# Eight neighbouring rows per partition for the expert up matrices, and a feed-forward input in permuted column order

## What is computed

```python
def route(h_flat, w_router, b_router):
    s = jax.nn.sigmoid((h_flat @ w_router).astype(jnp.float32))
    ...                                   # best group of 4, its 2 best experts, weights w
    return jnp.sum(jax.nn.one_hot(idx, N_EXPERTS, dtype=jnp.float32) * w[..., None], axis=1)

def moe(h, w_router, b_router, w1_l, w3_l, w2_l):
    ...
        a = jnp.einsum('td,edf->tef', xc, w1_l)     # d = 1024, f = 512, 16 experts
        b = jnp.einsum('td,edf->tef', xc, w3_l)
        u = jax.nn.silu(a) * b * gc[..., None]
        return jnp.einsum('tef,efd->td', u, w2_l)
...
        hx = rmsnorm(x, norm_ffn[l]) * (1 + sc_f) + sh_f
        x = x + g_f * moe(hx, w_router, b_router, w1[l], w3[l], w2[l])
```

## Time and profile before

| what | us |
|---|---|
| three runs | 1323.61, 1327.61, 1328.58 |
| median | 1327.61 |
| span of the profiled execution, first to last instruction | 1325.8 |
| PE busy | 1081.6 (82%) |
| DVE busy | 345.4 (26%) |
| ACT busy | 208.4 (16%) |
| queue of SP: share of the sixteen DMA engines | 58.9% |
| chain that ended last: PE 56%, DMA 29% (`ring<-in_w` alone 23%) | |

### The profile page before, as it was taken

One profiled execution on the slowest core, in us unless ns is written; L12 is line 12 of the kernel. 1 busy time (PEld: TensorE's weight loads), 2 busy tenths in 40 slices (PEclk: granted clock), 3 DMA queues, 4 the chain that ended last, 5 costly groups with the idle time before them and its releaser, 6 DMA issues.

```text
span 1325.8 us, 18500 instructions
## 1 busy us (share of the span) xinstructions
PE 1081.6 (82%) x6246; PEld 604.7 (46%) x6247; DVE 345.4 (26%) x812; ACT 208.4 (16%) x487; POOL 79.0 (6%) x126
## 2 busy tenths in 40 slices
PE   2799989988981999999899189989892898788771
PEld 1446447765450544444346044647642454344430
DVE  2201147565342100101011430157624011000002
ACT  1110023432010111111101211023300111011001
POOL 2000000001002000000000300000101000000001
PEclk8899999989985999999999689999985799999896
DMA  9923116576135899999369671313645699999993
GB/s 330 374 91 127 64 70 238 202 258 226 43 131 208 319 396 395 398 397 384 122 227 397 214 269 64 127 64 128 240 158 198 234 332 397 396 396 397 397 397 110
DMA packets 142294, 328.60 MB, mean 248 GB/s; under 512 B 6552, under 2 KB 8760, under 8 KB 142240
## 3 DMA queue, kind: packets, MB, share of 16 engines
q1 hardware_dynamic: 125424, 287.84, 58.9%
q0 software_dynamic: 7856, 25.61, 5.4%
q10 hardware_dynamic: 8960, 14.40, 3.1%
HBM read 308.10 MB, written 19.73 MB: 247 GB/s over the span
## 4 chain that ended last, share of the span: by engine, by line
PE 56%; DMA 29%; DVE 7%; ACT 3%; issue 3%; POOL 2%; SPq 0%; ACTq 0%; DVEq 0%; POOLq 0%
DMA ring<-in_w 23%; PE S L1217 17%; PE S L1398 10%; PE S L1327 6%; PE O L1281 4%; PE T L1155 3%; PE AUX L1172 3%; DMA ring<-in_w_ada 3%; PE S L1432 2%; PE T L1432 2%; PE S L1248 2%; PE S L1402 2%; ACT R L643 1%; PE S L1437 1%; DVE R L916 1%
## 5 line engine op out<-in xcount | busy, mean ns | idle before, releaser
L1217 PE MATMUL S<-ring,hT 128*128 128x512 f32 (+1 forms) x576 | 226.0, 548 | 2.3 <-ACT hT L587 2.3
L1402 PE MATMUL S<-ring,R 128*64 128x256 f32 x1472 | 181.1, 405 | 33.0 <-DMA ring<-in_w 28.3
L1402 PEld LDWEIGHTS S<-ring,R 128*64 128x64 f32 x1472 | 114.5, 146 | 106.3 <-DMA ring<-in_w 40.3
L1217 PEld LDWEIGHTS S<-ring,hT 128*128 128x128 f32 x576 | 108.0, 191 | 104.3 <-issue 98.6
L1398 PE MATMUL S<-ring,R 128*128 128x512 f32 x320 | 144.1, 610 | 6.5 <-issue 3.3
L1155 PE MATMUL T<-cst,R 128*128 128x128 f32 (+1 forms) x497 | 80.1, 292 | 64.2 <-DVE R L793 30.4
L1088 DVE SCALAR_TENSOR_TENSOR R<-R,S 128x256 f32<-128x256 f32 (+1 forms) x33 | 16.6, 502 | 412.7 <-ACT R L694 412.7
L1155 PEld LDWEIGHTS T<-cst,R 128*128 128x128 f32 (+1 forms) x497 | 60.2, 151 | 93.4 <-DVE R L793 30.7
L1398 PEld LDWEIGHTS S<-ring,R 128*128 128x128 f32 x320 | 62.1, 195 | 87.2 <-issue 82.4
L1437 PE MATMUL S<-ring,R 128*64 128x512 f32 x368 | 84.0, 598 | 9.6 <-DMA ring<-in_w 5.7
L1327 PE MATMUL S<-ring,hT 128*128 128x512 f32 x192 | 85.6, 607 | 2.3 <-issue 2.3
(11 more groups left out here) (143 smaller groups left out, 756.8 us busy)
## 6 DMA issues: line engine op xcount, KB each, us to landing
ring<-in_w SPq DMA_DIRECT2D x96, 2048.0 KB, 11.5
ring<-in_w_ada SPq DMA_DIRECT2D x24, 2048.0 KB, 8.1
ring<-in_w_in SPq DMA_DIRECT2D x8, 2048.0 KB, 10.8
R<-x_d POOLq DMA_DIRECT2D x45, 256.0 KB, 5.7
ring<-in_w_out SPq DMA_DIRECT2D x4, 2048.0 KB, 9.8
R<-mod_d SPq DMA_DIRECT2D x12, 512.0 KB, 9.6
y_d<-R ACTq DMA_DIRECT2D x46, 128.0 KB, 5.3
y_d<-R ACTq DMA_DIRECT2D x20, 256.0 KB, 6.5
```

The lines of the kernel that those rows point to most:

```text
L1217: ins = pe.matmul(S[:, i % 4, 0:width], hT[:, k, t * P:(t + 1) * P], w[:, k, :], start=(k == 0), stop=(k == KC - 1))
L1402: ins = pe.matmul(S[64 * h:64 * h + 64, i, 0:256], xT[:, half, k % 4, k // 4, 0:64], part[i][:, k, h * 256:h * 256 + 256], start=(k == 0), ...
```

## The change

Three edits. `expert_src` gives w1 and w3 with row 8p + k at partition p, place k: a partition gets eight neighbouring rows, one run of 16 KB. w2 is as it was. `wr` is loaded by the same rule, a run of 512 B per partition. And `ffn_input` writes hb so that column 128k + i holds feature 8i + k: it reads X, Af and Bf with a step of eight floats (32 B) and writes hb contiguously; the second operation reads hb contiguously. All that comes behind it (transposes, scatter, fetch, products) takes hb by chunks and is unchanged. X, Af, Bf and the output of the experts keep their order.

Each engine has the same instructions in the same order before and after. Only the shape of the SP loads of w1 and w3 (128x8x512 becomes 128x4096), that of the wr load (128x8x16 becomes 128x128), and the access patterns of L978 and L979 differ.

```diff
@@ expert_src @@
                 one = w[l, ds(e, 1)].rearrange("a k n -> (a k) n")
+            if part < 2:
+                return one.rearrange("(p k) n -> p k n", p=P)
             return one.rearrange("(k p) n -> p k n", p=P)
@@ block.scalar @@
-            act.dma_start(wr[:, :, :], a["w_router"].rearrange("(k p) n -> p k n", p=P)).then_inc(s["router_in"], 16)
+            act.dma_start(wr[:, :, :], a["w_router"].rearrange("(p k) n -> p k n", p=P)).then_inc(s["router_in"], 16)
@@ ffn_input @@
                     for h in (0, 1):
                         r = slice(512 * h, 512 * h + 512)
-                        ch.step(dve.scalar_tensor_tensor(hb[t][:, r], X[:, t, r], rstd[:, c0:c0 + 1], Af[:, t // LT, r], ALU.mult, ALU.mult))
-                        dve.tensor_tensor(hb[t][:, r], hb[t][:, r], Bf[:, t // LT, r], ALU.add).then_inc(s["h_ready"], 1)
+                        own = lambda ap: ap.rearrange("p (i k) -> p k i", k=KC)[:, 4 * h:4 * h + 4, :]
+                        hv = hb[t][:, r].rearrange("p (k i) -> p k i", k=4)
+                        ch.step(dve.scalar_tensor_tensor(hv, own(X[:, t, :]), rstd[:, c0:c0 + 1], own(Af[:, t // LT, :]), ALU.mult, ALU.mult))
+                        dve.tensor_tensor(hv, hv, own(Bf[:, t // LT, :]), ALU.add).then_inc(s["h_ready"], 1)
```

## The result

The changed kernel takes 1310.91 us (median of 4 runs, 1308.79 to 1312.15), the kernel before 1325.61 us on the same chip. The ratio is 0.9892, interval 0.9869 to 0.9915: 14.7 us or 1.1% faster. The prediction was 1317.6 us with a range from 1306 to 1331, a gain of 10.0 us. Sign and range hold; the gain came out larger.

A forecast was written before the change was run, and what follows sets the result against it. DMA alone was taken to bound layer 1's expert loop, PE nearly to bound layer 0's. Terms: -10.6 - 2.2 - 0.8 - 0.7 + 4.3 = -10.0 us, giving 1317.6 us, range 1306 to 1331.

The forecast's parts named there:

- What bounds: Expert loop of layer 1: its last 37 loads hang on DMA alone, so what they save is kept, 10.6 us.
- Price of a load: Loads of w1 and w3: fewer, longer packets save 0.44 us per load, 0.88 at the far end.
- Layer 0, first stretch: Loads up to w1 of wide expert e4: five up matrices save 2.2 us; PE's waits offer 3.0 us.
- Last stretch: Layer 0's last loads: four up matrices make 1.8 us, but PE's wait allows only 0.8 us saved.
- wr: Router matrix load at the start: longer packets let w_ada loads, which PE awaits, come earlier, saving 0.7 us.
- Strides: Feed-forward input on DVE: stepped reads double eight exposed operations, 533 ns more each, costing 4.3 us.
- Token rows: Expert fetches beside 16 KB packets land 2.0 us later than 5.7 us; issued an expert ahead, this costs nothing.
- A cut at 4 KB: Rival on w1 and w3 loads: runs are cut or gain ends at 4 KB, 1323.1 us; 0.22 with the cycle rule.
- Free strides: Rival on DVE's stepped reads: they cost nothing, with the same load savings, 1313.3 us; chance 0.20.
- No lever: Rival on w1 and w3 loads: run length doesn't matter or packets stay unchanged, 1331.2 us; chance 0.14.
- slow long packets: Rival on w1 and w3 loads: 16 KB packets are slow, 3.1 us more per load, about 1433 us; chance 0.07.
- The rule of cycles: Fixed overhead of about 3 cycles per packet: 0.21 us saved per load, 1324.3 us; 0.22 together with the 4 KB cut.

The follow-up runs named there:

- the kernel with short packets: The changed kernel with a gap of two floats behind each w1 and w3 row in the ring slots, making 2 KB runs again: 1326.06 us, ratio 0.9996.
- the stepped single-input probe: One of nine 512-element DVE operations added at the start of the kernel before, a copy read with a step of 8 floats: 0.62 us.

## Why the prediction held, step by step

- **What bounds.** Right: 12.5 of the 15.3 us between the two spans come from the last chain, all of its saving kept.
- **Price of a load.** The mechanism was right, a fixed price per packet. The term was mis-sized: 0.44 us per load, 0.52 measured (0.47 against the kernel with short packets). Taken from two short windows by their rates, 389 and 408 GB/s; the shares of the same windows gave 0.88, which was too much. Two windows of 3 and 4 us were a thin base for this.
- **Layer 0, first stretch.** 2.2 us said; the step is 3.5, of which 0.7 is clock. The 2.8 that are left are near the 3.0 of the waits, which was the cap. **Last stretch.** 0.8 said, 1.0 found.
- **wr.** 0.7 us said, 0.34 found where the load lands (0.43 between the first two traces), nothing at the end. The first projection started 0.3 us later in the changed kernel: its fourth product took 3.59 us instead of 2.85, at a granted clock of 0.50 instead of 0.71 from 36 to 44 us. I had counted a load's landing as the end's gain, though PE's clock rises in this very place.
- **Strides.** Direction and count of exposed operations right, size too high: 0.53 us per operation taken for a doubling, 0.395 found, 3.1 us instead of 4.3. L775, with 12 ns on 16 elements, comes to 0.75 ns per element, and 0.77 was measured, but that they agree is luck. L775 has a single tile as input and jumps to and fro (8 floats on, 7 back); by 0.75 ns the stepped single-input probe would take 0.48 + 0.38 = 0.87 us, and it took 0.62. And 12 ns is no more than small operations differ by in this trace: one with one element (L869) takes 153 ns, one with two (L896) 169. The row that was missing was a stepped operation with two tiles. The note on cachelines in the Trainium skill, page "SBUF — State Buffer", section "Door 1: The DMA port swizzle", has full rate need two hits on a 16-byte line, and fp32 stride by up to 4 for free. The probes agree that a step of 8 costs, and disagree on 4: 1.06 us, where a step of 2 takes 0.69.
- **Not foreseen.** The queue for w_out. Expert 0's loads stand ahead of it in SP's order, so faster expert loads shorten a wait in a stage that I had called untouched: 0.85 us, of which the projection behind it loses 0.56 again.
- **Token rows.** They land in 7.0 us by the page, 7.7 said, 5.7 before (5.9 with 4-KB and 6.4 with 8-KB packets beside them), and PE doesn't wait longer for them: 34.7 us in all, 34.8 before. Right.
- **Rivals.** A cut at 4 KB (1323.1): ruled out by the 16-KB packets and the row of chains. Free strides (1313.3): nearer to the measured time than the forecast, but for the wrong reason. No lever, and slow long packets: ruled out. The rule of cycles in the Trainium skill, page "DMA: Bandwidth & Descriptors", section "Why small descriptors are slow (HBM only)", gives 0.21 us per load by the prediction's estimate. The traces disagree: 0.52.

The sum again with what was measured: -12.5 - 2.8 - 1.0 + 0.3 + 3.1 - 0.85 = -13.8, and PE's clock makes the rest to -15.3 of this pair of executions, by what is left over and not by a measurement of its own. By the medians it was 14.7, and 1325.61 - 10.0 would have been 1315.6: the missing 4.7 us are 1.9 of loads in the chain, 1.2 of strides, 0.85 of w_out, less 1.0 for the start, and layer 0 with the clock.

## What to carry over

Where a stage hangs on weight loads at full DMA share, look at the bytes per packet: give each partition neighbouring rows, and put the matching permutation where it costs least, here in PE's reading of a transpose rather than in an exposed DVE operation. Price a run length from two lengths that are already in the trace, and extend it as a price per packet. And when loads get faster, look down the issue queue for what stands behind them in other stages.

## What was not expected of the hardware

- A 512-element fp32 sum of two tiles on DVE costs 0.69 us at steps of 1 and 2 floats and 1.02 to 1.08 us at 4, 8 and 16; a second stepped operand or a stepped output with stepped inputs costs nothing more. With one tile as input a step of 8 takes 0.62 us in all.
- PE's transposes take 0.74 us per four at a step of 8 B and 0.75 at 16 B instead of 0.66, and in a narrow expert the next instruction starts no later for it.
- An idle time of 1.35 to 2.7 us ahead of PE's output projection of layer 1 goes with 2.4 to 3.1 us more for its 64 matmuls, so taking the wait away altogether was worth more than its own length in that stage, while shortening it was not: the longest waits (2.73 and 2.30 us) go with 30.04 us, the shortest (1.35 and 1.59) with 30.75. All nine traces with the wait show it and neither of the two without it does; but the same product of layer 0 took 29.25 to 29.29 us in three traces without any wait. That the idle time brings the clock down is thus argued, not shown.
